# Reordering the head of two mixture-of-experts layers on one core: shared products in parts between the routing products, the last shared product behind the first unit of experts

## The reference

```python
scores = jax.nn.sigmoid((xf @ router_w).astype(F32))
sel_scores = scores + router_b.astype(F32)
...
_, topi = lax.top_k(jnp.where(emask, sel_scores, -jnp.inf), TOP_K)      # 6 of 64, from 4 of 8 groups
topw = jnp.take_along_axis(scores, topi, axis=1)
topw = topw / (jnp.sum(topw, -1, keepdims=True) + 1e-20) * ROUTED_SCALE
routed = routed_experts(xf, topi, topw, w_gate, w_up, w_down)
shared = (jax.nn.silu(xf @ sh_gate) * (xf @ sh_up)) @ sh_down
return (routed + shared).reshape(B, S, D)
```

## Time and profile before

| | |
|---|---|
| time, three runs | 2747.27, 2750.25, 2751.19 us; median 2750.25 |
| profiled execution | 2748.05 us, span of its instructions 2746.7 us |
| mean granted TensorE clock | 0.965 |
| PE busy, DVE, ACT, POOL | 93%, 33%, 17%, 3% of the span |
| moved by DMA | 667.14 MB, mean 243 GB/s |

### The profile page before, as it was taken

One profiled execution on the slowest core, in us unless ns is written; L12 is line 12 of the kernel. 1 busy time (PEld: TensorE's weight loads), 2 busy tenths in 40 slices (PEclk: granted clock), 3 DMA queues, 4 the chain that ended last, 5 costly groups with the idle time before them and its releaser, 6 DMA issues.

```text
span 2746.7 us, 45874 instructions
## 1 busy us (share of the span) xinstructions
PE 2542.7 (93%) x18572; PEld 1815.6 (66%) x18572; DVE 915.4 (33%) x2171; ACT 476.2 (17%) x1040; POOL 80.3 (3%) x85
## 2 busy tenths in 40 slices
PE   8999899999999899999999888989999999889888
PEld 6777678887777788888864344444888754444444
DVE  3456323333556323332332111112564321111113
ACT  3222301001222211001221011101332211101102
POOL 0000000000000000000000000000000000000000
PEclk9999999999999999999989999999999999999999
DMA  5222246663232357654639999998231469999994
GB/s 205 77 93 108 92 168 231 235 276 128 92 108 108 107 194 288 243 230 157 231 142 418 419 404 416 419 408 328 91 123 63 189 244 419 419 417 413 418 412 181
DMA packets 100604, 667.14 MB, mean 243 GB/s; under 512 B 15600, under 2 KB 17152, under 8 KB 22336
## 3 DMA queue, kind: packets, MB, share of 16 engines
q1 hardware_dynamic: 90736, 647.50, 59.6%
q0 software_dynamic: 9392, 16.54, 1.7%
q10 hardware_dynamic: 288, 0.31, 0.0%
HBM read 677.92 MB, written 4.19 MB: 248 GB/s over the span
## 4 chain that ended last, share of the span: by engine, by line
PE 78%; DMA 11%; DVE 4%; ACT 3%; issue 3%; SPq 1%; DVEq 0%; ACTq 0%
PE PS L555 74%; DMA wmoe<-in_experts 11%; PE PS L560 4%; ACT AR L2385 1%; SPq L3024 1%; SPq L3021 1%; ACT AR L2435 1%; DVE ST L1543 0%; ACT wmoe L2385 0%; ACT ST L2385 0%; DVE AR L1540 0%; DVE AR L1712 0%; DMA X<-in_xT 0%; DVE AR L1687 0%; ACT X L2385 0%
## 5 line engine op out<-in xcount | busy, mean ns | idle before, releaser
L555 PE MATMUL PS<-H,wdense 128*128 128x256 f32 (+1 forms) x3056 | 701.2, 389 | 9.5 <-DVE H L1575 3.6
L555 PEld LDWEIGHTS PS<-H,wdense 128*128 128x128 f32 x3056 | 578.2, 191 | 114.3 <-issue 13.8
L2385 ACT ACTIVATE AR<-PS 128x256 f32<-128x256 f32 (+8 forms) x467 | 204.5, 446 | 1475.5 <-PE PS L555 927.0
L555 PE MATMUL PS<-AR,wdense 128*128 128x256 f32 (+1 forms) x1920 | 438.4, 389 | 18.3 <-DVE AR L1734 11.2
L555 PE MATMUL PS<-AR 128*32 128x2 f32 (+13 forms) x3360 | 428.6, 344 | 26.0 <-ACT AR L2385 9.0
L555 PEld LDWEIGHTS PS<-AR,wdense 128*128 128x128 f32 x1920 | 368.4, 192 | 83.6 <-DVE AR L1734 12.0
L555 PE MATMUL PS<-wmoe,AR 128*32 128x256 f32 (+3 forms) x3200 | 318.5, 458 | 98.3 <-DMA wmoe<-in_experts 55.7
L555 PEld LDWEIGHTS PS<-AR 128*32 128x32 f32 (+6 forms) x3360 | 214.6, 140 | 164.3 <-issue 99.6
L555 PEld LDWEIGHTS PS<-wmoe,AR 128*32 128x32 f32 (+2 forms) x3200 | 157.7, 128 | 224.1 <-issue 176.8
L555 PE MATMUL PS<-wdense,AR 128*32 128x256 f32 (+6 forms) x2608 | 265.4, 427 | 4.2 <-ACT AR L2385 2.4
L555 PEld LDWEIGHTS PS<-wdense,AR 128*32 128x32 f32 (+3 forms) x2608 | 124.7, 118 | 117.3 <-issue 59.6
(11 more groups left out here) (280 smaller groups left out, 1246.8 us busy)
## 6 DMA issues: line engine op xcount, KB each, us to landing
wmoe<-in_experts SPq DMA_DIRECT2D x192, 1024.0 KB, 19.1
wdense<-in_dense SPq DMA_DIRECT2D x176, 1024.0 KB, 4.8
wdense<-in_experts SPq DMA_DIRECT2D x128, 1024.0 KB, 20.1
AR<-in_experts SPq DMA_DIRECT2D x64, 1024.0 KB, 20.9
wmoe<-in_ada SPq DMA_DIRECT2D x48, 1024.0 KB, 7.7
tokens<-AR POOLq DMA_DIRECT2D x4, 512.0 KB, 2.9
wdense<-in_dense SPq DMA_DIRECT2D x2, 768.0 KB, 9.5
CST<-in_late SPq DMA_DIRECT2D x1, 1428.0 KB, 6.0
```

The lines of the kernel that those rows point to most:

```text
L555: return te.matmul(out, lhsT, rhs, start=start, stop=stop, skip_group_check=True)
L2385: return ac.activation(dst, src, f, bias=bias, scale=scale)
```

## The change

On PE the shared gate and up products are cut into parts (`shared_part`, a range of k) and these stand between the routing products; they use banks 0 and 1 in place of 4 and 5. The counts wait for DVE's `selected` (the 0/1 matrix M_SEL) in place of `weights`. The shared down product and `more groups` go into `shared_down()`, which the first unit runs behind its `gate_up`, where the later units have the `down` of the unit before. The shared down weights get a place of their own in the arena (SHD) and are loaded by a DMA of their own. So the last four dense loads of a layer are other ones, and loads 8 to 11 of the ring wait for other products. DVE's set-up operations that need nothing of the router go ahead of its wait for the router, a memset of M_WTG and one comparison go, and DVE's order is changed to match PE's. SP's waits at the loop `more` are exact: on its first turn a load waits for the product that last read its own slot.

```diff
-            for bk in (4, 5):
...
-            slot = take(DC, 256)
-            for f in range(2):
-                m = shared_half(slot, 4, f)
-            PE.up(m, "shared gate up", L, 4)
-            used()
-            te.wait_ge(VE.sem, VE.of("weights", L))
+            gate = take(DC, 256)
+            shared_part(gate, 0, 0, 0, DC)
+            te.wait_ge(VE.sem, VE.of("selected", L))
...
+            te.wait_ge(VE.sem, VE.of("weights", L))
+            o = bank(("weights turned", L), AC)
...
+            shared_part(gate, 0, 1, 0, 2)
...
+            shared_part(gate, 0, 1, 2, 6)
+            settle(B_D[1])
             te.wait_ge(VE.sem, VE.of("chosen 0", L))
             numbers("numbers 0", L)
...
+            PE.up(shared_part(gate, 0, 1, 6, DC), "shared gate", L)
             used()
-            free = uses[0] - 4
+            up = take(DC, 256)
+            shared_part(up, 1, 0, 0, 4)
+            settle(B_D[0])
             te.wait_ge(VE.sem, VE.of("chosen 1", L))
             numbers("numbers 1", L)
...
+            shared_part(up, 1, 0, 4, DC)
+            shared_part(up, 1, 1, 0, 4)
...
                     down(last, slots, what + ("d",))
+                else:
+                    shared_down()
...
                 te.wait_ge(VE.sem, at(VE, what + ("hidden",)))
+                if not last:
+                    te.wait_ge(VE.sem, VE.of("entries", L))
...
             gather(0, ("first x0", L))
+            PE.up(shared_part(up, 1, 1, 4, DC), "shared up", L)
...
             gather(1, ("first x1", L))
-            te.wait_ge(VE.sem, VE.of("entries", L))
+            te.wait_ge(VE.sem, VE.of("excess", L))
...
+            def shared_down():
+                te.wait_ge(VE.sem, VE.of("more groups", L))
...
+                te.wait_ge(shared_down_landed, 16 * (L + 1))
...
+                if n == 8:
+                    sp.dma_start(SHD.rearrange("p k w -> p (k w)"), io["dense"][SHARED_DOWN + L]).then_inc(shared_down_landed, 16)
...
-                    sp.wait_ge(PE.sem, used(which, x, ("more", L)) - per + per * i)
+                    sp.wait_ge(PE.sem, before[j] + per * i + (i >= 1) * max(0, used(which, x, ("more", L)) - per - before[j]))
```

More of the change, by code:

```diff
@@ L1233, in moe_layer, with settle @@
             PE.up(m, "router", L)
-            held.extend((4, 5))
+            def settle(*banks):
+                for b in banks:
+                    for done, label in owed[b]:
+                        te.wait_ge(done.sem, done.of(*label))
+                    owed[b] = []
+            held.extend((0, 1))
             for t in range(2):
@@ L1283, in moe_layer @@
             PE.up(mm(o[:, 8 * UNITS:12 * UNITS], index, M_ONE[0:NE]), "by group", L)
+            te.wait_ge(AC.sem, AC.of("weights turned", L))
             o = bank(("group weights", L), AC)
             PE.up(by_group(o, 0, M_TURN[:, S:2 * S], M_ONE[0:NE]), "group weights", L)
[L1286 to L1292, removed]
-            def numbers(*label):
-                for t in range(2):
-                    for g in range(4):
-                        m = mm(PS[GROUP * g:GROUP * (g + 1), B_D[1], 0:2], M_PM[:, t, g, :], M_WC[:, t, g, :], start=t == 0, stop=t == 1)
-                PE.up(m, *label)
+            shared_part(gate, 0, 1, 2, 6)
+            settle(B_D[1])
             te.wait_ge(VE.sem, VE.of("chosen 0", L))
             numbers("numbers 0", L)
[L1303 to L1313, removed]
+            PE.up(shared_part(gate, 0, 1, 6, DC), "shared gate", L)
             used()
-            free = uses[0] - 4
+            up = take(DC, 256)
+            shared_part(up, 1, 0, 0, 4)
+            settle(B_D[0])
             te.wait_ge(VE.sem, VE.of("chosen 1", L))
             numbers("numbers 1", L)
[L1318 to L1322, removed]
+            shared_part(up, 1, 0, 4, DC)
+            shared_part(up, 1, 1, 0, 4)
             def gather(half, what):
@@ L2228, in moe_layer @@
             VE.up(ve.tensor_tensor(OFF, A, PAST, ALU.subtract))
+            ve.wait_ge(PE.sem, PE.of("numbers 1", L))
+            numbers(1, 1, first_numbered[L], "numbers 1", L)
             own()
@@ L2234, in moe_layer @@
             VE.up(ve.tensor_reduce(XE, M_ABOVE[0:NE], AX, ALU.add), "excess", L)
[L2236 to L2257, removed]
             ex, hb = M_EX[:, 0], M_EX[:, 1]
-            gp = PS[:, 4, :].rearrange("p (f s) -> p f s", f=2)
-            up = PS[:, 5, :].rearrange("p (f s) -> p f s", f=2)
+            gp = PS[:, 0, :].rearrange("p (f s) -> p f s", f=2)
+            up = PS[:, 1, :].rearrange("p (f s) -> p f s", f=2)
             ve.wait_ge(AC.sem, AC.of("shared sigmoid", L))
@@ L2263, in moe_layer @@
             own()
-            ve.wait_ge(PE.sem, PE.of("shared gate up", L, 5))
+            ve.wait_ge(PE.sem, PE.of("shared up", L))
             VE.up(ve.tensor_tensor(hb, ex, up, ALU.mult), "shared hidden", L)
[L2266 to L2270, removed]
             o = PS[:, B_D[0], :]
@@ L2827, in moe_layer @@
                     copy(("ht", L, t, q), M_HT[:, t, 512 * q:512 * q + 512], ps("ht", L, t, q))
-            copy(("turned", L), M_TURN[0:NE], ps("turned", L)[0:NE])
-            ac.wait_ge(PE.sem, PE.of("shared gate up", L, 4))
-            AC.up(act(M_EX[:, 0], PS[:, 4, :].rearrange("p (f s) -> p f s", f=2), Sigmoid), "shared sigmoid", L)
-            ac.wait_ge(VE.sem, VE.of("groups cleared", L))
+            copy(("turned", L), M_TURN[0:NE, 0:S], ps("turned", L)[0:NE, 0:S])
+            copy(("weights turned", L), M_TURN[0:NE, S:2 * S], ps("weights turned", L)[0:NE, 0:S])
             copy(("group weights", L), M_WTG[:, :, 0:4 * UNITS], ps("group weights", L)[:, 0:8 * UNITS].rearrange("p (t g) -> p t g", t=2))
@@ L3067, in moe_layer @@
             turns = sp.value_load(NTI[0:1, L:L + 1], min_val=1, max_val=1 + NOV // 2)
+            before = [used(w0, x0, ("units", L, o0 + (w0 == 2))) + PE.turns_of("units", L) * (BODIES - 2) for w0, o0, x0 in BODY_LOADS[-RING:]]
             with sp.Fori(0, turns) as i:
```

119 lines of the change are left out of this document (84 added, 35 removed).

## The result

The changed kernel took 2730.27 us (median of six runs, 2726.45 to 2738.33) and the kernel before, measured with it, 2748.86 (2747.22 to 2751.19): a ratio of 0.9938, 95% interval 0.9922 to 0.9954, so 13 to 21 us faster.

The account below looks back on a forecast made before the run. PE's order bounds the head, the expert-weight stream the units. Waits and slow clock, 13.6 us, less 1.4 for turns and 0.6 for the fetch, give 11.6 us faster: 2738.5 us, range 2734 to 2747.

Parts of the forecast that it names:

- The heads: Shared gate product to second unit's gate product, each layer: removed waits and slow clock win 7.4 and 6.2 us before charges.
- the DMA engines pause: After loads 12 to 15, until the second unit frees slots: a new pause of some 7 us.
- the pauses at the new turns: PE's some seven more switches between kinds of product in the head: 0 to 2.3 us a layer, taken as 0.7.
- a tie: Ahead of x0: tokens landed at 1404.5, PE ready at 1405.0; 0.3 us a layer charged.
- the rival in which the fetch lands late: Tokens land late ahead of x0, PE idles and the clock falls: at 10.4 us landing, 7.9 us slower, 2758; 5%.
- I therefore carry the head's gain to the layer's end one for one: From the second unit on: load 16 some 8 to 9 us sooner, PE 7.4; same program, only shifted.
- the rival's mark: Ahead of x0: 2 us of PE idle, from a landing of about 7.2 us on, where the gain is gone.
- the two terms that stood at nothing in it: The units behind the head and the rest of the program: the sum gave neither any gain.
- kept their clock: Rival: clock falls once in each layer's cut head, 1.4 us faster, 2749, no change; 12% with smaller mishaps.
- The rule of the Trainium skill: In the finely cut head, short idles between matmul groups going round PSUM banks can make the clock swing between two levels.
- The stream does not set all: Rival that the weight stream sets all: each layer gains the 15.7 us by which load 12 moves, 2719; 3%.
- The exact waits at the last units: At the loop `more`: last loads go a unit sooner, costed at nothing; otherwise up to 4.6 us a layer gained.

Follow-up runs that it names:

- the stream late: Changed kernel with load 12 held back behind the shared down product, PE's order untouched: 2739.48 us, and 2740.03 in a second trace.
- after again: The changed kernel run a second time with no edit: 2732.49 us against 2744.87 for the kernel before (0.9946).

## Why the prediction was right and wrong

**The heads: right.** Forecast 6.4 and 5.2 us, 11.6 together; measured 6.8 and 4.0 in the first pair of traces, and 10.9 between the mean heads (90.1 us of two traces before, 79.2 of three after). The waits and the slow clock named in the sum are gone. From gate product to first unit the way is 12.9 us shorter in the first layer (forecast 12.7) and 9.8 in the second (forecast 11.2), where the fetch's wait is new; the first unit takes 7.13 us; the DMA engines pause around 1425. With the fetch's wait taken out the second head saves 44.2 - 38.2 = 6.0 of the 6.2 us in its sum, and in the first layer 7.4 - 6.8 leaves 0.6 for pauses, fetch and the 0.48 us that is still there ahead of the first unit. So the pauses at the new turns cost little.

**The first fetch: mis-sized.** I charged 0.3 us a layer for a tie. It is a tie in the first layer (landing 4.1 us); in the second it landed in 7.2 us, and PE waited 1.75, 2.25 and 1.63 us in the three traces of the changed kernel. That is the small form of the rival in which the fetch lands late. It didn't decide, since the clock stayed up: the gathers behind this wait take 0.63 and 0.60 us. That was in part luck. In the first trace with the stream late the wait at this place was 2.17 us, and behind it the granted clock fell to 0.66 from 2210 to 2215:

```profile
2209.43 0.63 PE L563 MATMUL PS<-CST,AR 128*128 128x128 f32 x4 [2.17 <-DMA AR<-tokens,IX]
...
2212.49 1.06 PE L563 MATMUL PS<-CST,AR 128*128 128x128 f32 x4
```

The second gather took 1.06 us for 0.60 and that head 41.9 us, which makes up nearly all of that trace's 1.7 us. Behind the 2.25 us in the second trace of the changed kernel the clock stayed at 1.00. So an idle of some 2 us, the rival's mark, is followed by a fall in one execution and not in another.

**"I therefore carry the head's gain to the layer's end one for one": the step that failed.** The same paragraph had load 16 flowing 8 to 9 us sooner and PE 7.4, and I dropped the difference. Before, by that count, loads 12 to 15 were still in flight when the second unit freed the next slots; with 8.2 us more of lead they are done by then (the pause, 0.39 from 1420 to 1430: in the first layer the last of them landed 9.7 us behind the second unit's start before, and 1.2 us ahead of it after), and PE, which does wait for the stream from some 40 us on, gets its weights sooner. The landings bear this out: load 16 is issued 4.4 us behind the second unit's start in both kernels, and from there it took 7.7 us (first layer) and 6.9 (second) to land before, and 6.1 and 4.8 after. Over all five traces it is 7.4 against 5.6 us on average, 1.8 us a layer that the stream gained beyond PE. Holding load 12 back, at the same order of PE, shows that the units depend on the lead. The change is worth about 3 us there: 972.6 (mean of two traces before) against 969.4 (mean of three after). So 10.9 + 3.2 = 14.1 us is what the runs can put down to the change; it lies within the intervals of all three measurements, but under each of their middles (17.0, 14.8 and 16.5 us by their ratios; the plain differences of the medians are 18.6, 12.4 and 17.8). What lies between, up to 3 us, is not put down to anything here.

**The range: the scatter was mis-sized.** The units' 3.2 us alone would have left the time in the range: 2738.5 - 3.2 = 2735.3. For the scatter I allowed 2 us, from three runs that spread over 4. In the first pair of traces the rest of the program gave 1683.5 - 1678.9 = 4.6 us of its own, 3.4 of it ahead of the first layer's gate product (1388.63 - 1385.26). The 18.0 us between these spans are thus 10.9 in the heads, 2.5 in the units and 4.6 in the rest, which I take for scatter: the second trace of the changed kernel has 10.4 us more of it than the first. Against the sum's 11.6 us that is 0.7 less in the heads, 2.5 and 4.6 more in the two terms that stood at nothing in it, so the larger part of the miss in that pair is chance. The kernel before has medians from 2743.85 to 2750.25 in this study; the forecast was set off from the highest.

**The rivals.** The cut heads of the first trace after kept their clock: 1.00 from 1390 to 1440 and from 2190 to 2230. The rule of the Trainium skill weighed in the prediction (TensorE: Matmul & The Clock Gate, "A second HAM failure mode: psum-queue depth-cycling") did not show in them, at any of these small products. The stream does not set all: the 15.0 and 12.2 us by which load 12 moves in the two layers, measured from the gate product, became 1 to 2 us a layer in the units, not the whole. The exact waits at the last units won nothing that could be measured, as forecast.

## What to carry to other kernels

Where two engines take turns at being waited for, a gain on one is not simply carried on: compare how far each moves against the next place where it is waited for, and keep the difference as a term. A delay put on one of them alone (one wait more) measures how much lead the other needs, better than any reading of one trace. Before a small gain is sized, read two traces of the same kernel: what differs between them in code that nobody touched is the width of the range.

## What was not expected of the hardware

Code that no version changes took other times from one execution to the next, and in the pair of traces below the granted clock went with it. From the first layer's last down product to the second layer's router, traces took 263.3 to 270.6 us. In windows of the same stretch, after (263.6) and after again (270.6, its program about 1 us later there):

```profile
2110.00:2130.00 20.00, 19.05 (x224) 15.47 (x219) 9.06 (x15) 7.69 (x16) 0.00 (x0) 1.00 0.01 2
2130.00:2150.00 20.00, 17.77 (x72) 14.65 (x73) 3.03 (x8) 1.32 (x2) 0.00 (x0) 0.91 0.91 368
```

```profile
2111.00:2131.00 20.00, 19.89 (x214) 16.98 (x216) 9.10 (x15) 5.81 (x12) 0.00 (x0) 0.83 0.01 2
2131.00:2151.00 20.00, 16.83 (x89) 13.19 (x88) 3.85 (x9) 3.78 (x7) 0.00 (x0) 0.83 0.71 289
```

The one ran at 1.00 and 0.91, the other at 0.83 twice. Why it falls in one execution and not in the other stays open; no run here was made for it.

A fetch beside one 1 MB load landed in 4.1 us in the first layer and in 7.2 us in the second, with the load issued 0.9 and 0.8 us behind it (7.7 and 7.1 in the second layer of the two further traces); alone it took 3.5 and 4.0.
